# A two-layer hybrid decoder trunk on one core: first stage and layers in one block, modulation dealt to two engines

## The chip, the cores and the metric

The kernel runs on one core of a Trainium2 chip. A core has TensorE (PE) for matmuls, VectorE (DVE) and ScalarE (ACT) for elementwise work, GpSimd (POOL), and SyncE (SP), which issues most transfers; 16 DMA engines move the data. Each engine has its own queue of instructions, worked off in order, and waits on semaphores for the others. The metric is the device time of one execution in microseconds. The kernel before took 2327.58 us, the median of 3 runs (2323.72 to 2328.54).

## The reference

A trunk of two layers on x (1024 tokens, 1024 channels, float32). Before the layers, c gives six modulation vectors per layer; the first two (shift and scale of the first norm) are needed before anything else of a layer:

```python
ang = positions.astype(jnp.float32)[..., None] * inv_freq     # rotary angles
c_act = jax.nn.silu(c)
for l in range(DEPTH):                                        # 2 layers
    mod = c_act @ ada_w[l] + ada_b[l]                         # 1024 x 6144 weights
    sh1, sc1, g1, sh2, sc2, g2 = split(mod, 6)
    h = rmsnorm(x, norm1_g[l]) * (1.0 + sc1) + sh1
    proj = h @ w_in[l]
    y = concat(ssd_mixer, mla_mixer, swa_sink_mixer)(proj) @ w_out[l]
    x = x + g1 * y
    h = rmsnorm(x, norm2_g[l]) * (1.0 + sc2) + sh2
    u = causal_dwconv(h @ ffn_w_up[l])
    a, b = split(u, 2)
    x = x + g2 * ((silu(a) * b) @ ffn_w_down[l])
return rmsnorm(x, final_norm_g)
```

## The kernel before

Activations lie transposed on chip (channels on the 128 partitions, tokens along the row), as 8 tiles of 128 channels. A dense product of two float32 operands is made of three products of rounded parts: each operand is split into a high part (a copy by ACT) and a low part (a subtraction by POOL or DVE), and PE multiplies high by high, high by low and low by high. The weights of the input projection come in 20 packs of 128 columns, each loaded into one of two buffers (raw) and split. Everything is ordered by counted semaphores; the waits are written out by hand. In the layers a wait is given as `nth(name, v)`, v more than the count with which the layer began.

The program has three parts. The **first stage** is a block of its own. SP loads c, the rotary constants, the positions, the 8 tiles of x, tiles 0 to 7 of the modulation weights (`adaw`, 128 x 1024 each, 512 KB: tile i = 8 g + k holds rows 128 k to 128 k + 127 of vector g), then 16 narrow parameter loads (`load_params`, L394), tiles 8 to 15, and the first two packs of the input projection (`load_win`, L440); pack 0 consists of four narrow pieces. PE turns c, then the tiles of x one after another (L545), the copies out of its memory being made by ACT (L571); then it turns the parameters (L412 to L417), which waits for all 16 loads. ACT also squares x (L584), computes the sines (L586) and the roots of the norm (L588), and copies the parameters (L423). DVE computes the rotary angles (L606 to L617), then multiplies the modulation tiles by the silu of c and adds them up: tiles 1 to 7 into one sum, 9 to 15 into another (L625, L628). Tiles 0 and 8 are multiplied by PE itself, as products with one column (`part_sums`, L553), which also adds up the partitions of DVE's two sums in the same way. Between the two sums PE spreads the roots of the norm with 8 transposes (`spread_rms`, L453). DVE ends the stage with small additions (L638 to L641) and `first_modulation` (L431, L433). The two packs are split at the end (`split_ahead`, ACT L449, POOL L446).

The **second part** is a block in which the five engines clear the semaphores of the first. A block ends with all engines meeting. The **third** holds both layers (`trunk_layer`). Layer 0 starts with DVE's scaled norm (L2128), ACT's high part (L1743) and DVE's low part (L2136) of one channel tile after another, and PE's products of packs 0 and 1 with them (L1127), then packs 2 to 19 (L1067). SP's queue of layer 0 starts with eight further modulation tiles (L788), pack 2 and pack 3, and the store of x (L825).

Of the kernel before, what the change touches and what calls it, by code (L numbers as in the profile page):

```python
# [31 lines left out]
F32 = mybir.dt.float32  # L32
# [6 lines left out]
P = 128  # L39
T = 1024  # L40
# [89 lines left out]
ADA_GROUP = [0, 0, 1, 1, 2, 2, 3, 3, 4, 4, 4, 5, 5, 5, 6, 6]  # L130
# [47 lines left out]
def pv_end(u):  # L178
# [24 lines left out]
    "cum_stored": 16, "cum_loaded": 128, "ada_early_loaded2": 64, "sd_xe": 7, "sd_xe0": 1, "sd_t": 2, "sd_c": 4,  # L203
# [8 lines left out]


# [4 lines left out]
def build(nc, x, c, positions, ada_w, ada_b, norm1_g, norm2_g, w_in, ssd_conv_w, ssd_conv_b,  # L218
# [248 lines left out]
    adas = [place(f"adas{g}", [P, D], F32, E[(12, 13, 15)[g]]) for g in range(3)]  # L467
# [8 lines left out]
    with ExitStack() as st:  # L476
        s = sems(st, [f"x_loaded{t}" for t in range(NB // 2)] + [f"ada_loaded{i}" for i in range(7)] + ["small_loaded", "ident_ready", "pool_step", "x_transposed",
                      "x_copied_act", "x_copied_dve", "c_transposed", "c_act", "angle", "rope_sin",
                      "ada_done", "ada_sum", "dve_step", "params_loaded", "params_transposed", "params_copied", "mod_first",
                      "next_loaded0", "next_loaded1", "next_hi", "next_lo", "n1_sq", "n1_rstd", "n1_spread"])  # L480
        with nc.Block() as block:

            @block.sync
            def _(sp):
                sp.dma_start(crow[:], c.rearrange("b (k p) -> (b k) p", p=P)).then_inc(s["small_loaded"], 16)
                sp.dma_start(ropec[:], rope_consts).then_inc(s["small_loaded"], 16)
                sp.dma_start(posi[64:128, :], positions.to_broadcast([64, T])).then_inc(s["small_loaded"], 16)
                def load_adaw(i):
                    g, k = divmod(i, KT)
                    sp.dma_start(adaw[i][:], ada_w[0, k * P:(k + 1) * P, g * D:(g + 1) * D]).then_inc(s[f"ada_loaded{ADA_GROUP[i]}"], 16)  # L490

                for t in range(NB):
                    sp.dma_start(xin[t][:], x[0, t * P:(t + 1) * P, :]).then_inc(s[f"x_loaded{t // 2}"], 16)
# [11 lines left out]
            @block.gpsimd  # L505
            def _(pool):

                pool.memset(ident[:], 0.0).then_inc(s["pool_step"], 1)
                pool.memset(band[:], 0.0).then_inc(s["pool_step"], 1)
                pool.memset(caus01[:], 1.0).then_inc(s["pool_step"], 1)  # L510
                pool.memset(cs[0:64, :], 0.0).then_inc(s["pool_step"], 1)
                pool.memset(eps, EPS).then_inc(s["pool_step"], 1)
                pool.wait_ge(s["pool_step"], 5)
                pool.affine_select(out=ident[:], in_=ident[:], compare_op=ALU.not_equal, fill=1.0, base=0,
                                   pattern=[[-1, P]], channel_multiplier=1).then_inc(s["ident_ready"], 1)

                pool.affine_select(out=band[:, 0, :], in_=band[:, 0, :], compare_op=ALU.is_gt, fill=NEG, base=0,
                                   pattern=[[1, P]], channel_multiplier=-1).then_inc(s["ident_ready"], 1)

                pool.affine_select(out=band[:, 1, :], in_=band[:, 1, :], compare_op=ALU.is_ge, fill=NEG, base=0,  # L520
                                   pattern=[[-1, P]], channel_multiplier=1).then_inc(s["ident_ready"], 1)
                pool.affine_select(out=caus01[:], in_=caus01[:], compare_op=ALU.is_ge, fill=0.0, base=0,
                                   pattern=[[1, P]], channel_multiplier=-1).then_inc(s["ident_ready"], 1)
                for n in range(AHEAD):
                    split_ahead(pool, n)

            def x_copied(eng, t):

                if t < X_ACT:
                    eng.wait_ge(s["x_copied_act"], t + 1)  # L530
                else:
                    eng.wait_ge(s["x_copied_act"], X_ACT)
                    eng.wait_ge(s["x_copied_dve"], t + 1 - X_ACT)

            @block.tensor
            def _(pe):
                pe.wait_ge(s["ident_ready"], 4)
                pe.wait_ge(s["small_loaded"], 48)
                pe.transpose(bank[3][:, 0:8], crow[:], ident[0:8, 0:8]).then_inc(s["c_transposed"], 1)
                for t in range(NB):  # L540
                    pe.wait_ge(s[f"x_loaded{t // 2}"], 32)
                    if t >= 2:
                        x_copied(pe, t - 2)
                    for k in range(KT):
                        mm = pe.transpose(bank[t % 2][:, k * P:(k + 1) * P], xin[t][:, k * P:(k + 1) * P], ident[:])  # L545
                    mm.then_inc(s["x_transposed"], 1)
                x_copied(pe, NB - 1)
                transpose_params(pe, prow)

                def part_sums(a, column, weights):  # L550

                    for m in range(KT):
                        last = pe.matmul(bank[3][:, 16 + column + m:17 + column + m], a[:, m * P:(m + 1) * P], weights,  # L553
                                         start=True, stop=True)
                    last.then_inc(s["ada_sum"], 1)

                pe.wait_ge(s["c_act"], 1)
# [9 lines left out]
            def copy_x(eng, t, sem):  # L567
                eng.wait_ge(s["x_transposed"], t + 1)
                src = bank[t % 2][:].rearrange("p (k t) -> p k t", k=KT)
# [2177 lines left out]
```

## Time and profile before

| | before |
|---|---|
| median of 3 runs | 2327.58 us (2323.72 to 2328.54) |
| the profiled execution's own time | 2329.56 us |
| its span, first to last instruction | 2327.1 us |
| busy: PE, DVE, ACT, POOL | 2264.4, 1628.7, 1098.3, 1008.1 us |
| granted clock of PE, mean | 0.990 |
| first layer's first norm product | starts at 49.27 us |
| first dense product | starts at 51.61 us |

Times in the profile are microseconds from the start of the span unless they are marked as ns. L12 is line 12 of the kernel before. In a row of the timeline the start and the duration come first; `x16` means that 16 like instructions were merged, the duration then being from the start of the first to the end of the last; in square brackets stands how long the engine had been idle and what ended that. PEld is the loading of weights into PE. A granted clock of 1.00 is 2.4 GHz, 0.50 is 1.2 GHz.

### The profile page before, as it was taken

Reading aid. Unit: us, or ns where it says so; the run is one execution under the profiler, and the core shown is the slowest. Engines: PE = TensorE matmul, PEld = TensorE weight load, DVE = VectorE, ACT = ScalarE, POOL = GpSimd, SP = SyncE. Lnnn points to the kernel's source line nnn. Section 1 sums busy time; section 2 is a strip of 40 time slices with the busy share of each in tenths; the row PEclk is TensorE's granted clock in tenths of the full one; section 3 lists DMA queues with packets and bytes.
Section 4 is the critical chain, followed back from the end, with each engine's and each line's share of the span. In section 5 each row is a group of like instructions: output and inputs, shape, how many; then the busy total and the mean of one; then the engine's idle time right before and its main releaser. Section 6 shows DMA issues by size and latency. Waiting matters only on the chain.

```text
span 2327.1 us, 30806 instructions
## 1 busy us (share of the span) xinstructions
PE 2264.4 (97%) x11289; PEld 1833.2 (79%) x11289; DVE 1628.7 (70%) x2095; ACT 1098.3 (47%) x1808; POOL 1008.1 (43%) x641
## 2 busy tenths in 40 slices
PE   6999999999899999999999999999989999999998
PEld 5888866787788888888878787668878888888887
DVE  6885458449876666777888744672796767677886
ACT  4345546434444444444543464662444444444455
POOL 1222377444987777300012124043389777760000
PEclk7999999999999999999999999999999999999999
DMA  8742323342333333487557131004313333347763
GB/s 292 281 151 62 88 64 110 109 127 73 93 116 96 117 98 117 149 286 253 153 215 245 55 81 51 1 30 171 118 55 113 113 91 114 91 131 259 257 208 113
DMA packets 273012, 311.08 MB, mean 134 GB/s; under 512 B 37033, under 2 KB 191647, under 8 KB 271839
## 3 DMA queue, kind: packets, MB, share of 16 engines
q1 hardware_dynamic: 272174, 307.94, 40.7%
q8 instruction: 90, 1.47, 0.3%
q10 hardware_dynamic: 688, 1.18, 0.2%
q14 instruction: 60, 0.48, 0.1%
HBM read 246.53 MB, written 61.49 MB: 132 GB/s over the span
## 4 chain that ended last, share of the span: by engine, by line
PE 85%; DVE 7%; issue 2%; ACT 2%; POOL 1%; DMA 0%; DVEq 0%; SPq 0%; ACTq 0%; POOLq 0%
PE bank L1497 31%; PE bank L1067 18%; PE bank L1512 17%; PE bank L1127 6%; PE bank L1328 2%; PE bank L1360 1%; PE bank L1288 1%; DVE hLo L2150 1%; PE bank L1388 1%; DVE xT L2144 1%; PE bank L1217 1%; DVE xT L2472 1%; DVE tLo L2541 1%; ACT swaProb L1872 1%; PE bank L1195 1%
## 5 line engine op out<-in xcount | busy, mean ns | idle before, releaser
L987 POOL TENSOR_TENSOR wLo<-raw,wHi 128x1024 fp32r<-128x1024 f32 x66 | 161.5, 2448 | 411.4 <-ACT wHi L989 411.4
L1690 POOL TENSOR_TENSOR prodLo<-comb,prodHi 128x512 fp32r<-128x512 f32 x160 | 234.0, 1470 | 122.0 <-ACT prodHi L1029 122.0
L1497 PE MATMUL bank<-tHi,prodHi 128*128 128x512 f32 x640 | 249.9, 390 | 5.7 <-DVE tLo L2541 4.2
L1497 PE MATMUL bank<-tLo,prodHi 128*128 128x512 f32 x640 | 249.1, 389 | 0.0
L1497 PE MATMUL bank<-tHi,prodLo 128*128 128x512 f32 x640 | 249.1, 389 | 0.0
L1512 PE MATMUL bank<-gateHi,downHi 128*128 128x512 f32 x616 | 240.3, 390 | 0.0
L1512 PE MATMUL bank<-gateHi,downLo 128*128 128x512 f32 x616 | 239.7, 389 | 0.0
L1512 PE MATMUL bank<-gateLo,downHi 128*128 128x512 f32 x616 | 239.7, 389 | 0.0
L1029 ACT ACTIVATE prodHi<-comb 128x512 fp32r<-128x512 f32 x160 | 100.9, 634 | 249.0 <-PE bank L1497 228.7
L2486 DVE SCALAR_TENSOR_TENSOR ub<-bank,ffp,ub 128x1023 f32<-128x1023 f32 x88 | 112.8, 1282 | 141.9 <-ACT ub L1958 140.3
L1497 PE MATMUL bank<-hHi,prodHi 128*128 128x512 f32 x480 | 187.1, 390 | 7.1 <-POOL prodLo L1690 4.5
L1497 PE MATMUL bank<-hHi,prodLo 128*128 128x512 f32 x480 | 186.8, 389 | 0.0
L1497 PE MATMUL bank<-hLo,prodHi 128*128 128x512 f32 x480 | 186.7, 389 | 0.0
L1067 PE MATMUL bank<-hHi,wHi 128*128 128x512 f32 x576 | 184.8, 402 | 0.0
L1067 PE MATMUL bank<-hLo,wHi 128*128 128x512 f32 x576 | 178.2, 391 | 0.0
L1067 PE MATMUL bank<-hHi,wLo 128*128 128x512 f32 x576 | 177.5, 389 | 0.0
L989 ACT ACTIVATE wHi<-raw 128x1024 fp32r<-128x1024 f32 x66 | 69.7, 1059 | 219.1 <-PE bank L1067 144.5
L1690 POOL TENSOR_TENSOR prodLo<-raw,prodHi 128x512 fp32r<-128x512 f32 x120 | 165.0, 1405 | 0.0
L1497 PEld LDWEIGHTS bank<-tHi,prodHi 128*128 128x128 f32 x640 | 120.1, 188 | 33.1 <-DVE tLo L2541 5.0
L1497 PEld LDWEIGHTS bank<-tHi,prodLo 128*128 128x128 f32 x640 | 120.1, 188 | 25.2
L1497 PEld LDWEIGHTS bank<-tLo,prodHi 128*128 128x128 f32 x640 | 120.1, 188 | 24.8
L1512 PEld LDWEIGHTS bank<-gateHi,downHi 128*128 128x128 f32 x616 | 115.6, 188 | 24.4 <-issue 0.8
(393 smaller groups left out, 5346.4 us busy)
## 6 DMA issues: line engine op xcount, KB each, us to landing
raw<-in_ffn_w_up_dram SPq DMA_DIRECT2D x88, 512.0 KB, 4.8
gateRaw<-gateOut SPq DMA_DIRECT2D x154, 256.0 KB, 4.2
adaE<-in_ada_w_dram SPq DMA_DIRECT2D x64, 512.0 KB, 6.5
gateOut<-gateSums SPq DMA_DIRECT2D x22, 1024.0 KB, 5.5
raw<-in_w_in_dram SPq DMA_DIRECT2D x34, 512.0 KB, 4.1
downRaw<-in_ffn_w_down_dram SPq DMA_DIRECT2D x66, 256.0 KB, 3.8
raw<-in_w_out_dram SPq DMA_DIRECT2D x28, 512.0 KB, 3.8
downCols<-in_ffn_w_down_dram SPq DMA_DIRECT2D x24, 512.0 KB, 3.6
```

The source lines that it names most:

```text
L987: eng.tensor_tensor(lo[:], raw[slot][:], fview(hi[:]), ALU.subtract).then_inc(s["split_lo"], 1)
L989: eng.activation((early_hi if n in (N_OUT0, N_PRE + 2) else third_hi if n == 2 else wHi[slot])[:], raw[slot][:], ACT.Copy).then_inc(s["spl ...
L1029: act.activation(sHiW[idx][:], product_source(js, idx), ACT.Copy).then_inc(s["us_hi"], 1)
L1067: last = mm(half(pair, hf), w(k), r(k)[:, HALF * hf:HALF * (hf + 1)], start=first and q == 0, stop=last_k and q == 2)
L1127: last = mm(o, w[n % 2][:, k * P:(k + 1) * P], r(k)[:, cols], start=first and q == 0, stop=last_k and q == 2)
L1195: last = mm(half(3, 0)[:, g * 256:(g + 1) * 256], bt[:, g, :], xe[:, 4 * g:4 * g + 4, :], start=True, stop=True)
L1217: last = mm(o, xd[:, h, :], Mt[g][:, q, :], start=True, stop=True)
L1328: last = mm(bank[u % 2][:, q * HALF + a:q * HALF + b], qh[h][0:96, i * BLK:n], kh[h][0:96, a:b], start=True, stop=True)
L1497: last = mm(o, w[idx][:, c0], moving(idx, kp, hi), start=kp == 0 and q_ == 0, stop=kp == 3 and q_ == 2)
L1512: last = mm(down_bank(p, m), w[ring(n)][:, m * P:(m + 1) * P], g[ring(n)][:], start=i == 0 and q == 0, stop=i == NK - 1 and q == 2)
L1690: pool.tensor_tensor(sLoW[idx][:], product_source(js, idx), fview(sHiW[idx][:]), ALU.subtract).then_inc(s["us_lo"], 1)
L2486: dve.scalar_tensor_tensor(out=y[:, d:T], in0=bank[2 * q + b][:, 0:T - d], scalar=ffp[:, col:col + 1], in1=y[:, d:T], op0=ALU.mult, op1=AL ...
```

## The change

1. The first stage becomes a function, `first(block)`, that is called in the same block as the two layers; the block that cleared the semaphores is gone, and so are the ends of two blocks. The first stage uses semaphores of the layers under other names (`FIRST_ON`), and the layers count on from what it has left in them (`FIRST`, `passed`).
2. SP no longer issues the positions, the 16 parameter loads and pack 0; GpSimd's queue does, after its nine constants and before its splits. SP issues x, the 16 modulation tiles without a break, and pack 1.
3. Each modulation tile has its own semaphore. PE multiplies tiles 1, 3, 5, 7, 9, 11, 14 and 15; the eight transposes of `spread_rms` stand ahead of tile 9 in its queue. DVE multiplies and adds 0, 2, 4, 6 into one sum, 8, 10, 12, 13 into another, folds each by a 32 x 32 transpose and a reduction, and PE finishes the fold with four narrow products.
4. In layer 0 SP waits for the first modulation before the eight further modulation tiles. PE waits for the low part of pack 0 before its first product and of pack 1 before the second tile's, in both layers; SP's loads of packs 2 and 3 wait for the splits of packs 0 and 1 one by one. The early tiles' six semaphores become two.

```diff
-ADA_GROUP = [0, 0, 1, 1, 2, 2, 3, 3, 4, 4, 4, 5, 5, 5, 6, 6]
+ADA_BY_PE = (1, 3, 5, 7, 9, 11, 14, 15)
+ADA_BY_DVE = (0, 2, 4, 6, 8, 10, 12, 13)
...
 # SP, first stage
-                sp.dma_start(posi[64:128, :], positions.to_broadcast([64, T])).then_inc(s["small_loaded"], 16)
...
-                for i in range(8):
-                    load_adaw(i)
-                load_params(sp, lambda w: w[0:1], prow)
-                for i in range(8, 2 * KT):
-                    load_adaw(i)
-                for n in range(AHEAD):
-                    load_win(sp, w_in[0:1], n, n, s[f"next_loaded{n}"])
+            for i in range(2 * KT):
+                load_adaw(i)
+            load_win(sp, w_in[0:1], 1, 1, s["next_loaded1"])
...
 # GpSimd, after its constants
+            pool.dma_start(posi[64:128, :], positions.to_broadcast([64, T])).then_inc(s["pos_loaded"], 16)
+            load_params(pool, lambda w: w[0:1], prow)
+            load_win(pool, w_in[0:1], 0, 0, s["next_loaded0"])
...
 # PE, after the parameters' transposes
                 pe.wait_ge(s["c_act"], 1)
-                for g in range(2):
-                    pe.wait_ge(s[f"ada_loaded{ADA_GROUP[g * KT]}"], 16 * ADA_GROUP.count(ADA_GROUP[g * KT]))
-                    part_sums(adaw[g * KT], (2 + g) * KT, cact[:, 0:1])
-                pe.wait_ge(s["ada_done"], KT - 1)
-                part_sums(adas[0], 0, caus01[:, P - 1:P])
-                spread_rms(pe, "n1")
-                pe.wait_ge(s["ada_done"], 2 * KT - 2)
-                part_sums(adas[1], HALF, caus01[:, P - 1:P])
+            for n, i in enumerate(ADA_BY_PE):
+                if i == 9:
+                    spread_rms(pe, "n1")
+                pe.wait_ge(s[f"mod_loaded{i}"], 16)
+                part_sums(adaw[i], KT * n, cact[:, i % KT:i % KT + 1])
+            pe.wait_ge(s["ada_done"], len(ADA_BY_DVE) + 2)
+            for r in range(4):
+                last = pe.matmul(bank[0][32 * r:32 * r + 32, 0:2 * KT], quad[:], foldP[:].rearrange("p j c -> p (j c)")[:, r:2 * 32:4],
+                                 start=True, stop=True)
...
 # DVE
+            for n, i in enumerate(ADA_BY_DVE):
+                g, k = divmod(i, KT)
+                dve.wait_ge(s[f"mod_loaded{i}"], 16)
...
+                if n % 4 == 3:
+                    dve.wait_ge(s["ada_done"], n + 1 + g)
+                    link(dve.transpose(nt[2][:], adas[g][:]))
+                    dve.tensor_reduce(foldP[:, g, :], nt[2][:].rearrange("p (c i) -> p c i", i=32), AX.X, ALU.add).then_inc(s["ada_done"], 1)
...
+            dve.wait_ge(s["ada_sum"], len(ADA_BY_PE))
+            link(dve.tensor_reduce(mod[:, 0:2 * KT].rearrange("p (g m) -> p g m", g=2),
+                                   bank[3][:, 16:16 + KT * len(ADA_BY_PE)].rearrange("p (g n m) -> p g m n", g=2, m=KT), AX.X, ALU.add))
+            dve.wait_ge(s["params_copied"], 1)
+            link(dve.tensor_tensor(mod[:, 0:2 * KT], mod[:, 0:2 * KT], prm[:, R_ADAB:R_ADAB + 2 * KT], ALU.add))
+            dve.wait_ge(s["ada_sum"], len(ADA_BY_PE) + 1)
+            link(dve.tensor_tensor(mod[:, 0:2 * KT], mod[:, 0:2 * KT], bank[0][:, 0:2 * KT], ALU.add))
...
 # layers
-                if layer and n < AHEAD + 2:
-                    sp.wait_ge(s["next_hi"], nth("next_hi", 0))
-                    sp.wait_ge(s["next_lo"], nth("next_lo", 0))
+                if n < AHEAD + 2:
+                    sp.wait_ge(s["next_hi"], nth("next_hi", n - AHEAD - 1))
+                    sp.wait_ge(s["next_lo"], nth("next_lo", n - AHEAD - 1))
...
+                    else:
+                        sp.wait_ge(s["mod_first"], nth("mod_first", 0))
                     load_early(0, range(KT), 0)
...
-            if layer:
-                pe.wait_ge(s["next_lo"], nth("next_lo", 0))
...
+                if k == 0:
+                    pe.wait_ge(s["next_lo"], nth("next_lo", t - 1))
...
+    with nc.Block() as block:
+        first(block)
+        s.update(own)
+        passed.update(FIRST)
+        for layer in range(DEPTH):
+            trunk_layer(block, layer)
```

## Rows read from the trace of the kernel before

**Rows 1.** The page, part 4: the chain that ended last, by engine.

```profile
PE 85%; DVE 7%; issue 2%; ACT 2%; POOL 1%; DMA 0%; DVEq 0%; SPq 0%; ACTq 0%; POOLq 0%
```

**Rows 2.** The chain of waits from 0 to 130 us: start, duration, what.

```profile
51.61 24.81 PE bank L1127 x96
```

**Rows 3.** The timeline of DVE and POOL, end of the first stage.

```profile
42.91 4.66 POOL L446 TENSOR_TENSOR wLo<-raw,wHi 128x1024 fp32r<-128x1024 f32 x2 [39.31 <-ACT wHi L449]
...
46.59 0.16 DVE L641 TENSOR_TENSOR mod<-mod,bank 128x8 f32<-128x8 f32 x1 [3.45 <-PE bank L553]
46.79 0.81 DVE L431 TENSOR_TENSOR mod<-mod,prm 128x16 f32<-128x16 f32 x1
47.63 0.17 DVE L433 SCALAR_TENSOR_TENSOR scl<-mod,prm 128x8 f32<-128x8 f32 x1
49.27 1.40 DVE L2128 SCALAR_TENSOR_TENSOR nt<-xT,scl,bank 128x512 f32<-128x512 f32 x2 [1.48 <-PEq L645]
```

**Rows 4.** The timeline of SP and ACT, first 26 us.

```profile
1.68 0.57 SPq L487 DMA_DIRECT2D posi<-in_positions_dram  x1
...
23.82 1.05 ACT L571 ACTIVATE xT<-bank 128x1024 f32<-128x1024 f32 x1
...
25.93 1.05 ACT L586 ACTIVATE nt<-nt 64x1024 f32<-64x1024 f32 x1
```

**Rows 5.** The timeline of PE, 29 to 47 us.

```profile
29.22 0.44 PE L412 MATMUL bank<-ident,paramRows 121*128 121x121 f32 x1 [6.25 <-DMA paramRows<-in_ssd_a_log_dram]
...
30.83 6.99 PE L553 MATMUL bank<-cact,adaw 128*128 128x1 f32 x32
...
41.09 1.95 PE L453 MATMUL bank<-ident,rst 128*128 128x128 f32 x8
...
42.91 3.57 PE L553 MATMUL bank<-caus,adas 128*128 128x1 f32 x16
```

**Rows 6.** The timeline of DVE, 15 to 43 us.

```profile
15.30 0.69 DVE L617 TENSOR_SCALAR nt<-nt 64x1024 f32<-64x1024 f32 x1
...
20.95 8.23 DVE L628 SCALAR_TENSOR_TENSOR adas<-adaw,cact,adas 128x1024 f32<-128x1024 f32 x6 [1.73 <-DMA adaw<-in_ada_w_dram]
32.22 0.75 DVE L625 TENSOR_SCALAR adas<-adaw,cact 128x1024 f32<-128x1024 f32 x1 [3.03 <-DMA adaw<-in_ada_w_dram]
...
36.02 6.84 DVE L628 SCALAR_TENSOR_TENSOR adas<-adaw,cact,adas 128x1024 f32<-128x1024 f32 x5 [0.87 <-DMA adaw<-in_ada_w_dram]
```

**Rows 7.** Stretches: length; busy of PE, PEld, DVE, ACT, POOL; granted clock; DMA; GB/s.

```profile
408.50:411.90 3.40, 3.39 (x27) 2.68 (x27) 1.51 (x4) 1.62 (x5) 3.32 (x3) 0.99 0.00 0
411.90:415.10 3.20, 3.20 (x22) 2.42 (x24) 1.85 (x4) 1.50 (x2) 3.20 (x2) 0.50 0.00 0
...
19.30:22.70 3.40, 3.24 (x16) 2.83 (x15) 1.63 (x2) 3.40 (x6) 0.00 (x0) 0.50 1.03 410
22.70:26.40 3.70, 0.27 (x2) 0.00 (x0) 3.49 (x3) 3.68 (x7) 0.00 (x0) 0.96 1.04 354
...
30.80:46.50 15.70, 15.68 (x74) 15.31 (x74) 9.56 (x11) 2.73 (x6) 3.59 (x2) 0.50 0.74 225
```

**Rows 8.** The timeline of PE at 182 us and at 409 us.

```profile
182.72 0.30 PE L1144 MATMUL bank<-foldMod,quadSum 128*32 128x32 f32 x8
...
409.08 1.92 PE L1136 MATMUL bank<-caus,nt 128*128 128x1 f32 x16
410.86 0.96 PE L1360 MATMUL bank<-ident,prob 128*128 128x128 f32 x7
```

**Rows 9.** The timeline of DVE at 96 us: the transpose of one fold.

```profile
95.73 1.21 DVE L2197 STREAM_TRANSPOSE foldTurned<-nt 128x1024 f32<-128x1024 f32 x1
```

**Rows 10.** SP's parameter issues: timeline, then the line's groups (ns min/median/max).

```profile
20.44 0.59 SPq L394 DMA_DIRECT2D paramRows<-in_ssd_a_log_dram  x1
...
L394 SPq DMA_DIRECT2D paramRows<-in_norm_g_dram x2: 335/1034/1733, 11.6 to 12.0; - x2
...
L394 SPq DMA_DIRECT2D paramRows<-in_mla_q_norm_g_dram x1: 247/247/247, 15.3 to 15.3; - x1
```

More of the change, by code:

```diff
@@ L211 @@
     "dn_used": 69, "dn_full": 28, "dn_free": 16}
+FIRST_ON = {
+    "small_loaded": ("k_rope", 32), "ident_ready": ("up_base", 4), "pool_step": ("up_tap", 5),
+    "x_loaded0": ("gk_loaded0", 32), "x_loaded1": ("gk_loaded1", 32), "x_loaded2": ("gk_loaded2", 32), "x_loaded3": ("gk_loaded3", 32),
+    "x_transposed": ("up_silu", NB), "x_copied_act": ("up_mul", X_ACT), "x_copied_dve": ("g_sums", NB - X_ACT),
+    "c_transposed": ("dn_c", 1), "c_act": ("dn_copied", 1), "angle": ("dn_u", 1), "rope_sin": ("dn_pre", 1),
+    "ada_done": ("dn_used", 10), "ada_sum": ("us_c", 9)}
+FIRST_ON.update({f"mod_loaded{i}": (name, 16) for i, name in enumerate(
+    "dc_loaded0 dc_loaded1 dc_loaded2 g_stored0 g_stored1 g_stored2 x_back x_saved tail_loaded0 tail_loaded1 "
+    "sd_row_stored sd_spread uproj_loaded cum_stored dt_stored dt_loaded".split())})
+FIRST = {"dve_step": 16, "params_transposed": 1, "params_copied": 4, "mod_first": 1, "next_loaded1": 16, "next_hi": 2, "next_lo": 2,
+         "n1_sq": NB, "n1_rstd": 2, "n1_spread": 1}
+FIRST.update({name: count for name, count in FIRST_ON.values()})
 R_N1, R_N2, R_ADAB, R_CW, R_CB, R_SN, R_QN, R_KN, R_FN, R_DT, R_END = 0, 8, 16, 64, 96, 104, 108, 110, 111, 119, 121
@@ L466, in build @@
     adaw = [place(f"adaw{i}", [P, D], F32, at["h"] + 4 * K * i) for i in range(2 * KT)]
-    adas = [place(f"adas{g}", [P, D], F32, E[(12, 13, 15)[g]]) for g in range(3)]
+    adas = [place(f"adas{g}", [P, D], F32, E[12 + g]) for g in range(2)]
+    foldP = place("foldFirst", [P, 2, 32], F32, E[15])
     two_pi = 6.283185307179586
@@ L684, in build @@
         up_base up_tap up_silu up_mul g_stored0 g_stored1 g_stored2 g_sums gk_loaded0 gk_loaded1 gk_loaded2 gk_loaded3 dc_loaded0 dc_loaded1 dc_loaded2 dn_c dn_copied dn_u dn_pre g_hi g_lo dn_used dn_full dn_free""".split()
+    names += "turned x_gained made_act made_dve out_written".split()
+    held = ExitStack()
+    s = sems(held, names + ["first_pos", "first_params", "first_win0"])
+    own = {n: s[n] for n in s}
+    s.update({signal: own[name] for signal, (name, count) in FIRST_ON.items()})
@@ L1234, in scan_after @@
                         6: [(scan_back, ch)] + ([(scan_turn, ch + 1)] if ch + 1 < NB else [])}
[L1236 to L1237 removed]
             for t, k in [(t, k) for t in range(2) for k in range(4)] + [(t, k) for k in range(4, KT) for t in range(2)]:
[L1239 to L1240 removed]
+                if k == 0:
+                    pe.wait_ge(s["next_lo"], nth("next_lo", t - 1))
+                    if layer:
+                        pe.wait_ge(s["dn_free"], nth("dn_free", -1 if t else -3))
                 pe.wait_ge(s["n1_lo"], nth("n1_lo", n1_done(0, k)))
@@ L2238, in key_rope @@
                     rope(dve.tensor_tensor(misc[a, :], misc[a, :], misc[b, :], ALU.add), 3)
-            early_products(0, range(KT), 0, KT)
+            early_products(0, range(KT), 0)
             step_sum()
@@ L2243, in _ @@
             mod_fold(0)
-            early_products(1, range(KT), 1, KT)
+            early_products(1, range(KT), 1)
             mod_fold(1)
@@ L2268, in _ @@
                 if j == 0:
-                    early_products(2, range(4), 2, 4)
+                    early_products(2, range(4), 2)
                 if j == 1:
@@ L2700, in _ @@
                 made_by_dve(6)
-    names += "turned x_gained made_act made_dve out_written".split()
-    with ExitStack() as st:
-        s = sems(st, names)
-        with nc.Block() as block:
-            for layer in range(DEPTH):
-                trunk_layer(block, layer)
-                for name, count in PER_LAYER.items():
-                    passed[name] = (layer + 1) * count
+    with nc.Block() as block:
[4 more added lines that the diff above has]
+            trunk_layer(block, layer)
+            for name, count in PER_LAYER.items():
+                passed[name] = FIRST.get(name, 0) + (layer + 1) * count
 _INS = ["x", "c", "positions", "ada_w", "ada_b", "norm1_g", "norm2_g", "w_in", "ssd_conv_w", "ssd_conv_b",
```

294 lines of the change are left out of this document (132 added, 162 removed), and 3 rows, old and new, of the table PER_LAYER.

## The prediction

> **What bounds the kernel now.** I read the page first, then the chain of waits from the start, then the first 60 us of the timeline engine by engine, and last the granted clock in stretches of that time. The page's chain lies on TensorE (PE) for 85% of the span [rows 1]. The chain from the start shows where PE takes over: at 51.61 us the first dense products begin and PE goes on without a gap for 24.81 us, and then with the next packs [rows 2]. So whatever the first stage takes is added to the span whole: no engine has slack behind 51.61 us that could swallow it. The change is almost all in front of that point, and I measure it by one moment, the start of VectorE's (DVE's) first norm product (L2128), at 49.27 us before [rows 3]. From there to the first dense product is 2.34 us of DVE, ScalarE, DVE, which the diff leaves alone.
>
> What comes before 49.27: DVE sums 14 of the 16 tiles of the modulation weights (tiles 9 to 15 wait for their transfers, 3.03 us and 0.87 us, the last five go through by 42.86) [rows 6]; PE turns the second sum in 16 one-column passes, 42.91 to 46.48 [rows 5]; DVE closes with three small operations; then 1.48 us of nothing until L2128, which is the end of the block, the clearing of the semaphores and the second end [rows 3]. Two of the terms are known at sight: the barriers, 1.48 us, and 0.64 us of L431, which took 0.81 us for 16 columns and ended at 47.60, when GpSimd's split (42.91 + 4.66 = 47.57) let go [rows 3].
>
> **The change part by part.**
>
> *Barriers.* Gone: -1.48 us. Counted offsets cost nothing: the same waits with other constants. L2128 waits for mod_first and n1_spread, both signalled just before.
>
> *Modulation on PE.* This is the large term. PE had 2 of the 16 tiles and two turned sums; it now has 8 tiles. One tile is 8 products, and each is two passes of a weight load and a one-column matmul: 32 passes for two tiles took 6.99 us, so 3.5 us a tile; the two sums of 16 passes took 3.57 us the second time, the same [rows 5]. DVE pays 1.37 us for such a tile (6 in 8.23 us) [rows 6]. Eight tiles on PE are 28.0 us in one queue, in order. PE cannot start them before it has transposed x and the parameters. The last copy of x that it waits for ends at 23.82 + 1.05 = 24.87 us; without the positions' issue in front of x (0.57 us on SP's queue) it is 24.3 [rows 4]. Then:
>
> - parameters ready: 25.2, see below
> - their transposes: 29.19 to 30.83 before, 1.64 us [rows 5]: 26.8
> - tiles 1, 3, 5, 7: 14.0: 40.8. All landed (DVE ran through 0 to 7 by 29.2 [rows 6])
> - the eight turns of the norm's roots now stand in the middle of PE's queue, 1.9 us [rows 5]: 42.7. Their input, the reciprocal behind tile 8, is there by 33
> - tiles 9, 11, 14, 15: 14.0: 56.7. Tiles 11 to 13 had landed at 36.02, and DVE went on through 14 and 15 without a wait [rows 6], so no transfer ends last here
> - the fold of DVE's half, eight narrow passes: 0.30 us at 2.4 GHz for the like of it [rows 8], doubled for 1.2 GHz: 57.3
> - DVE's add and scale: 0.11 to start, 0.16, 0.04, 0.17 [rows 3], and L2128 follows: 57.8. The reduction of PE's 64 columns and the bias run beside the fold.
>
> 57.8 against 49.27: +8.5 us. The barriers and L431's stall are already in that difference.
>
> *The clock.* All of that stands on the 3.5 us of a tile, which is the price at a granted clock of 0.50 (1.2 GHz). At full clock 16 one-column passes took 1.78 us (409.08 to 410.86) [rows 8]. What would raise it? In 30.80:46.50 PE was busy 15.68 of 15.70 us, nearly all with such passes, and had 0.50 throughout. In 19.30:22.70 it was at 0.50 too, with full transposes, and had 0.96 behind that, in 22.70:26.40. In 408.50:411.90 PE was busy 3.39 of 3.40 us at 0.99, with 16 one-column passes in it, and had 0.50 in the 3.2 us behind [rows 7]. So one-column passes neither raised the clock nor held it. I take 0.50 from 26.4 us on, as before. A start of the parameters' transposes at full clock would give back up to 0.8 us.
>
> The Trainium skill, "TensorE: Matmul & The Clock Gate", Part 1, has the clock follow how busy the engine has been, and full rate come with sustained matmul activity. By that rule 28 us of matmuls without a gap would run at full rate and the change would win, as in the first rival below; this trace disagrees, with 15.68 us busy at 0.50.
>
> *DVE's half.* Eight tiles (2 x 0.75 + 6 x 1.37), two 32x32 transposes (1.21 us each [rows 9]) and two reductions of as many columns (taken the same), the scaled sines and the reciprocal: about 15.6 us. It starts behind DVE's chain for the sines, which ended at 15.30 + 0.69 = 16.0 [rows 6] and ends some 2 us later with later positions. Tile 13 is there at 36.0, then 1.3 + 2.4: finished at 40 to 43. PE needs it at 56.7, so it costs nothing; if PE were at full clock it would be late together with PE's own last tile.
>
> *Narrow transfers on GpSimd's queue.* Positions, 16 parameter loads and the four loads of weight pack 0 leave SP. Before, PE waited 6.25 us for the last parameter row, issued from 20.44 to 21.03 and landed by 29.2 [rows 5, 10]; that wait goes, which is in the sum. No row shows a DMA issued by GpSimd. Lower bound: SP's issues, 0.25 us the shortest; 17 of these from 3.6 us on land long before 24.3, and nothing is exposed. Upper bound: 1.73 us, the longest [rows 10], 17 times from 3.6, and 8.2 us to land: 41 us, 16 us late. I take the parameters at 25.2, nearest to SP's case (all 16 issued in the 9.4 us from 11.6 to 21.0 [rows 10]), with 0.9 us of exposure for a slower queue. Page price: the Trainium skill, "DMA: Bandwidth & Descriptors", gives about 1 us to the first byte on this path; by it 17 issues are out at 21 us and the sum is the one above. The positions only have to be in by 14 us, since ScalarE gets to the sines at 25.93 [rows 4] and DVE's chain in front of them is 10.7 us. Pack 0's slivers used to be in by 42, since GpSimd's share of the two splits ran from 42.91 for 4.66 us [rows 3]; the first product now starts at 60: over 12 us of cover. If they share the transfer engines with tiles 14 and 15, these may land at 42 to 44; PE reaches tile 14 at 49.7.
>
> *SP's queue in layer 0.* The wait for mod_first puts the eight early loads at the moment where the block used to put them, beside L2128; pack 2 and the store of x are queued behind them as before. No change relative to L2128. In layer 1 the looser waits on the split packs (one of two) release nothing that the chain waits for there. Shared semaphores for the early tiles: same order, same data.
>
> **Sum.** Profiled execution 2329.56 us, span 2327.1: +8.5 gives 2338 and 2335.6. The median of the three runs is 2327.58, 2.0 under the profiled one; to it the sum is 2336.1.
>
> **Rivals.**
> *1. PE's passes run at full clock (faster).* Start 25.2, transposes 0.9, four tiles 7.1, roots 1.0: 34.2; tiles 9 and 11: 37.8; 14 and 15: 41.4, or 43.4 if tile 15 lands at 41.6, when DVE read it; fold and close 0.8: 42.2 to 44.2, 5 to 7 us ahead of 49.27. 2321.5. For it: the queue has no gap, and the clock was high in 22.70:26.40. Against it: the two stretches with one-column passes [rows 7]. It decides as soon as the clock is high for more than about 60% of the 28 us; the break-even is 8.5 us saved of the 13.8 that full clock would save.
> *2. GpSimd's queue issues the 17 transfers late (slower still).* Over 1.2 us each, PE starts later than 25.2 one for one; at 1.73 us, 41 us, it is +24: 2352; at 1.4 us with 5 us to land, 32 us, +15.5: 2343. For it: 17 issues in a row on an engine whose price no row shows. Against it: SP's average of 0.59 us.
> The skill's "SBUF — State Buffer" (the trap of DVE blocking a GpSimd DMA) says that such a DMA stands still while DVE is in its two-port mode. No row here shows it; by it the issues beside DVE's fast operations from 6 to 18 us would be among the late ones.
> *3. No change.* PE gets a part of the time at full clock, some 40 to 60% of it, and the gain meets the loss: 2325 to 2331.
>
> **How the numbers follow.** Forecast 0.80, with its own range 2333.5 to 2341 (0.8 us of clock at the start, parameters from hidden to 5 us late). Rival 1: 0.09. Rival 2: 0.06. Rival 3: 0.05. About 0.2%, 4.7 us, is what a measurement can tell from no change here. The range leaves out rivals 1 and 3 and the far end of 2: 2332 to 2343. Faster 0.09, same 0.05, slower 0.86.
>
> **What would show it.** Right: PE busy without a gap from 25 to 57 us at a granted clock of 0.50, 16 passes in 3.5 us; L2128 at about 58 us; DVE's last fold at 40 to 43; no idle DVE between L433's like and L2128; the chain behind the first dense product shifted by a constant. Wrong: a clock of 1.00 in 27:57, a PE that waits for parameters beyond 27 us, or a first dense product that waits for pack 0.

## The result, and the profile after

The changed kernel takes 2331.91 us (median of 20 runs, 2328.77 to 2336.78), the kernel before 2325.62 on the same chip (20 runs, 2322.66 to 2331.80). The ratio is 1.0023, 95% interval 1.0016 to 1.0031: slower by 5.3 us, or by 6.3 us if the medians are subtracted. The prediction said slower, 2336.1 us in 2332.0 to 2343.0; the time lies 0.09 us below the range. The profiled execution of the changed kernel took 2330.20 us, with a span of 2328.2.

The moment by which the prediction measured, the first norm product (L2128), moved from 49.27 us [rows 3] to 55.53, by 6.26 us, where 8.5 was forecast. First the timeline of PE in the changed kernel, 21 to 56 us (start, duration, line, operation, output and inputs; in brackets the idle time before it and what ended it), which answers to [rows 5]:

```profile
23.80 0.32 PE L425 MATMUL bank<-ident,paramRows 121*128 121x121 f32 x1 [2.75 <-ACT xT L600]
...
25.27 13.82 PE L580 MATMUL bank<-cact,adaw 128*128 128x1 f32 x64
38.94 1.95 PE L466 MATMUL bank<-ident,rst 128*128 128x128 f32 x8
40.68 13.65 PE L580 MATMUL bank<-cact,adaw 128*128 128x1 f32 x64
54.26 0.30 PE L592 MATMUL bank<-foldFirst,quadSum 128*32 128x16 f32 x8
```

This is the queue that the prediction wrote down, without a gap from 23.80 to 54.5 us: parameters, four tiles, the eight turns, four tiles, the fold. Their order and kind are right, and each is a little shorter than forecast. The first row shows that the transposes of the parameters wait for ScalarE's copy of x, and no longer for a parameter row (before, 6.25 us for the transfer [rows 5]).

The stretches (length; busy time of PE, PEld, DVE, ACT, POOL; granted clock; DMA share; GB/s), answering to [rows 7]:

```profile
19.30:22.70 3.40, 1.06 (x8) 0.85 (x8) 3.30 (x4) 3.40 (x6) 0.00 (x0) 1.00 1.02 255
22.70:26.40 3.70, 2.60 (x25) 2.40 (x25) 2.35 (x3) 3.66 (x7) 0.00 (x0) 0.68 1.02 409
25.30:54.30 29.00, 29.00 (x142) 28.98 (x142) 14.00 (x13) 4.63 (x9) 4.70 (x2) 0.50 0.61 231
```

PE is busy 29.00 of 29.00 us and is granted 0.50 (1.2 GHz) all the while. Just before, in 19.30:22.70, it was at 1.00 with PE busy 1.06 of 3.40 us. The first rival needed full clock here and is out.

VectorE (DVE), its folds and its close, answering to [rows 3, 6]:

```profile
41.08 1.25 DVE L663 STREAM_TRANSPOSE nt<-adas 128x1024 f32<-128x1024 f32 x1
42.36 1.22 DVE L664 TENSOR_REDUCE foldFirst<-nt 128x32 f32<-128x1024 f32 x1
54.37 0.22 DVE L672 TENSOR_REDUCE mod<-bank 128x16 f32<-128x64 f32 x1 [10.79 <-PE bank L580]
54.63 0.17 DVE L675 TENSOR_TENSOR mod<-mod,prm 128x16 f32<-128x16 f32 x1
54.84 0.17 DVE L677 TENSOR_TENSOR mod<-mod,bank 128x16 f32<-128x16 f32 x1
55.04 0.17 DVE L678 SCALAR_TENSOR_TENSOR scl<-mod,prm 128x8 f32<-128x8 f32 x1
55.53 1.41 DVE L2128 SCALAR_TENSOR_TENSOR nt<-xT,scl,bank 128x512 f32<-128x512 f32 x2 [0.32 <-DVE scl L678]
```

DVE has finished its half at 43.58 and stands still for 10.79 us until PE has its last tile. That is the change in one number: half of the tiles went to the engine that needs 3.4 us for one, and the engine that needs 1.3 waits. The 1.48 us in front of L2128 [rows 3] are 0.32 now, and L431's 0.81 is 0.17.

GpSimd's queue, answering to [rows 10]; of the 16 parameter issues the first group and the last:

```profile
3.55 0.72 POOL L548 DMA_DIRECT2D posi<-in_positions_dram  x1
4.26 1.05 POOL L407 DMA_DIRECT2D paramRows<-in_norm_g_dram  x2
...
11.97 0.89 POOL L407 DMA_DIRECT2D paramRows<-in_ssd_a_log_dram  x1
12.85 4.10 POOL L453 DMA_DIRECT2D raw<-in_w_in_dram  x4
```

All 17 are out at 12.86 us, 0.55 us each, and the last parameter row lands 5.5 us after its issue, so the parameters are in long before PE asks for them.

**Only the first stage differs.** Before, the first dense product stood at 51.61 us [rows 2]; it is at 57.96 now. From there to the up-projection of the queries in layer 0 it is 258.27 us before and 258.19 after. Later in this pair of profiles the offset shrinks, to 5.0 us at the norm of layer 1 and to 1.1 us at the end of the span, while the medians of 20 runs each differ by 6.3: behind the first 310 us single executions part from each other by some us (from the up-projection to the end of the span the profiles of this document have 2011.6 to 2017.7 us), and a difference of 1.1 in two spans would have misled. So the experiments are compared by two things, their place at 310 us and their ratio over many runs.

### The profile page after: what moved, and what is told of

It is laid out like the page before. It is cut to its first block, busy times and chain, and to the rows that moved or that the text cites. A ratio compares the mean times of both kernels' runs of the same rounds, so it can differ in the third digit from the quotient of the medians.

```text
span 2328.2 us, 30890 instructions
## 1 busy us (share of the span) xinstructions
PE 2273.1 (98%) x11361; PEld 1843.8 (79%) x11361; DVE 1621.0 (70%) x2092; ACT 1096.3 (47%) x1808; POOL 1021.6 (44%) x662
## 4 chain that ended last, share of the span: by engine, by line
PE 87%; DVE 7%; ACT 2%; issue 2%; POOL 1%; DMA 1%; SPq 0%; DVEq 0%; ACTq 0%; POOLq 0%
PE bank L1497 31%; PE bank L1067 18%; PE bank L1512 18%; PE bank L1127 6%; PE bank L1328 2%; PE bank L1360 1%; PE bank L1288 1%; PE bank L580 1%; DVE hLo L2150 1%; PE bank L1388 1%; DVE xT L2144 1%; PE bank L1217 1%; DVE xT L2472 1%; DVE tLo L2541 1%; ACT swaProb L1872 1%
## 5 line engine op out<-in xcount | busy, mean ns | idle before, releaser
L1497 PEld LDWEIGHTS bank<-tHi,prodLo 128*128 128x128 f32 x640 | 120.4, 188 | 25.2
```

The source lines that it names most:

```text
L1497: last = mm(o, w[idx][:, c0], moving(idx, kp, hi), start=kp == 0 and q_ == 0, stop=kp == 3 and q_ == 2)
```

## The experiments

The times of each in one table. "Norm" is the start of the first norm product, "dense" that of the first dense product, "up" that of the up-projection of the queries in layer 0, all from one profile, in us.

| kernel | norm | dense | up | ratio to before, interval |
|---|---|---|---|---|
| before | 49.27 | 51.61 | 309.88 | 1 |
| changed | 55.53 | 57.96 | 316.15 | 1.0023 [1.0016, 1.0031] |
| e_blocks | 47.96 | 50.40 | 308.58 | 0.9992 [0.9983, 1.0002] |
| e_queue | 48.89 | 51.33 | 309.48 | 1.0002 [0.9993, 1.0011] |
| e_mod | 60.58 | 63.02 | 321.18 | 1.0041 [1.0027, 1.0054] |
| e_deal4 | 48.09 | 50.52 | 309.06 | 1.0006 [0.9997, 1.0014] |
| e_dense | 69.87 | 72.30 | 330.47 | 1.0078 [1.0059, 1.0097] |
| e_dense4 | 73.37 | 75.81 | 334.30 | one run, 2354.0 us |
| e_front4 | 46.44 | 49.10 | 307.39 | 0.9997 [0.9986, 1.0008] |
| e_front4p | 49.47 | 51.90 | 310.20 | 1.0004 [0.9992, 1.0015] |
| e_front4x | 47.41 | 49.85 | 308.24 | 0.9997 [0.9987, 1.0008] |
| e_port | 43.85 | 48.12 | 306.28 | 0.9989 [0.9978, 1.0000] |
| e_defer | 43.66 | 46.09 | 306.12 | 0.9994 [0.9985, 1.0003] |

"Up" minus "dense" is 258.15 to 258.54 in all but e_defer (260.03), so up to that point a shift of the first stage is carried on one for one. The shifts of "up" lie within the intervals of the ratios for all but two kernels: e_deal4 (-0.8 us, interval -0.7 to +3.3) and e_defer (-3.8, interval -3.5 to +0.7) are just outside. On the whole the times moved by somewhat less than the shifts. Why, stays open.

### The parts one by one: e_blocks, e_queue, e_mod

e_blocks keeps the joined block and puts the rest back: narrow transfers on SP, the old deal.

```
+            sp.dma_start(posi[64:128, :], ...)         # first on SP, as before
+            load_params(sp, ...)                       # behind tile 7, as before
-            for n, i in enumerate(ADA_BY_PE): ...
+            (two tiles and two turned sums on PE, 14 tiles on DVE, as before)
```

> The changed kernel with the narrow transfers back on SP's queue and the modulation dealt as before, so that only the joined block is left. Measure: start of the layers' first norm product on DVE (L2128 of before), 49.27 us before, 55.53 changed. Theory A (the 28 us of one-column passes in PE's queue at 1.2 GHz are the whole loss; joining the blocks gains the barriers): 47.8 us, time 1.5 us below before, ratio 0.9994. Rival B (GpSimd's queue is the loss): also 47.8, B is tested by the next run. Rival C (counting on shared semaphores in one block costs what the barriers did): 49.3 or more.

> The joined block and GpSimd's queue, modulation dealt as before (14 tiles on DVE, 2 on PE). A: parameters turned by 25.3 us, but DVE's sines now end at 23.0 instead of 16.0, so its 14 tiles run without waiting from 23.0 to about 43; first norm product at 47.5 (47 to 49), ratio 0.9993. B (the narrow packets slow the wide transfers, and DVE starts too late): 52 us or later, above before.

e_queue has the joined block and GpSimd's queue, with the old deal.

> The joined block and the new deal of the modulation, narrow transfers back on SP's queue. A: the parameters land at 29.2 us as before, and PE's queue starts from there: 29.2 + 1.6 + 14.0 + 1.9 + 13.8 + 1.2 = 61.7 us for the first norm product, ratio 1.0053; so the queue alone gained 6 us of what the deal lost. B: 55.5 us or less, since the slow queue is gone.

e_mod has the joined block and the new deal, with the narrow transfers on SP.

What was measured, by the start of the first norm product:

- the joined block alone: -1.31 us, as expected (47.96 for 47.8)
- GpSimd's queue on top of it: +0.93 with the old deal. A gain was expected (47.5, measured 48.89), since PE no longer waits for the parameters. That wait is gone, but the tiles land later, and DVE, which waits for them, now ends last (rows below). DVE also starts late: positions issued at 3.55 us beside the loads of x are waited for until 10.85, where SP's were there at 5.24. That is not what ends last, though, since DVE waits for transfers again behind its sines
- GpSimd's queue with the new deal: 60.58 to 55.53, -5.05, because PE is last in both and starts its tiles at 25.27 in place of 30.32
- the new deal: +12.62 without the queue, +6.64 with it

The wait for tile 10 and the tiles behind it, in e_blocks, then in e_queue:

```profile
32.49 1.28 DVE L658 SCALAR_TENSOR_TENSOR adas<-adaw,cact,adas 128x1024 f32<-128x1024 f32 x1 [0.42 <-DMA adaw<-in_ada_w_dram]
34.58 6.84 DVE L658 SCALAR_TENSOR_TENSOR adas<-adaw,cact,adas 128x1024 f32<-128x1024 f32 x5
...
35.33 1.28 DVE L656 SCALAR_TENSOR_TENSOR adas<-adaw,cact,adas 128x1024 f32<-128x1024 f32 x1 [0.40 <-DMA adaw<-in_ada_w_dram]
37.42 6.84 DVE L656 SCALAR_TENSOR_TENSOR adas<-adaw,cact,adas 128x1024 f32<-128x1024 f32 x5
```

Tile 10 comes 2.84 us later. Pack 0, 0.5 MB, now goes ahead of it, 1.3 us at the 410 GB/s that the loads reach. And while GpSimd's transfers run, the engines are as busy but move less: 322 GB/s in 8:12 us and 262 in 18:22, against 412 and 410 in e_blocks. How the 2.84 us divide between the two was not tested.

So the two edits can't be priced one at a time: the queue costs 0.9 or gives 5.1, by whether DVE's tiles or PE's end the stage. The new deal is the loss, in both settings.

### Fewer tiles on PE: e_deal4

```
-ADA_BY_PE = (1, 3, 5, 7, 9, 11, 14, 15)
+ADA_BY_PE = (1, 5, 11, 15)
+ADA_BY_DVE = (0, 2, 3, 4, 6, 7, 8, 9, 10, 12, 13, 14)
```

> The changed kernel with 4 tiles on PE (1, 5, 11, 15, the norm's spread ahead of 11) and 12 on DVE, six in each sum. A: PE has 7.0 us of passes less before the spread and again 7.0 behind it; tile 11 to 41.1, tile 15 to 44.6, DVE's second fold by 44.5; first norm product at 45.8 us (45 to 47.5), ratio 0.9985 to before. B: no better than 53 us, because the parameters and positions come as late as in the changed kernel.

The first norm product comes 7.4 us earlier than in the changed kernel, at 48.09. PE is done with its tiles at 45.63 in place of 54.33, although it now waits 4.22 us for DVE's reciprocal in front of the turns. So the price of a tile on PE is shown: four tiles less are 13.6 us less of passes. It is 2.3 us later than expected (and outside the 45 to 47.5), since DVE is now last. Rows of PE, then of DVE:

```profile
36.89 1.97 PE L466 MATMUL bank<-ident,rst 128*128 128x128 f32 x8 [4.22 <-DVE rst L670]
38.66 6.97 PE L580 MATMUL bank<-cact,adaw 128*128 128x1 f32 x32
46.95 0.31 PE L592 MATMUL bank<-foldFirst,quadSum 128*32 128x16 f32 x8 [1.32 <-DVE foldFirst L664]
...
31.75 1.78 DVE L658 SCALAR_TENSOR_TENSOR adas<-adaw,cact,adas 128x1024 f32<-128x1024 f32 x1 [1.51 <-DMA adaw<-in_ada_w_dram]
45.68 1.22 DVE L664 TENSOR_REDUCE foldFirst<-nt 128x32 f32<-128x1024 f32 x1
```

DVE's sines end at 22.22, but what holds it is again a transfer: the tile at the end of its first sum is there only at 31.75, takes 1.78 us in place of 1.28 beside GpSimd's split of pack 0 (29.24 to 32.45), and from there DVE works without a pause until its second fold ends at 46.90.

### What the clock does: e_dense and e_dense4

After each of PE's eight tiles one product, or four, that nothing reads:

```
                 part_sums(adaw[i], KT * n, cact[:, i % KT:i % KT + 1])
+                for _ in range(1):          # 4 in e_dense4
+                    pe.matmul(half(3, 1)[:, 0:512], ident[:], xin[0][:, 0:512], start=True, stop=True)
```

> The changed kernel with one matmul more after each of PE's eight modulation tiles: 128x512 fp32, a product that nothing reads, into a corner of bank 3. It asks whether columns that stream lift the granted clock that stands at 0.50 while PE is busy with one-column passes. If they do, the 16 passes (two tiles' worth of 64) cost 0.11 us a matmul and less from there on, tiles of 1.8 us with dense matmuls of about 0.9: PE's tiles end near 48 and the first norm product starts near 50. Rival: the clock stays at 0.50, each dense matmul adds 1.7 us at that clock, and the first norm product starts near 69, some 13 us after that of the changed kernel (55.5).

> The changed kernel with four matmuls of 128x512 after each of PE's eight tiles in place of one (nothing reads them): 7.3 us of streaming for each 3.4 us of one-column passes at half clock. If the share of streaming is what lifts the granted clock, it goes to 1.00 within the first tiles and the stage is shorter than at half clock: dense products of 0.9, passes of 1.8, first norm product between 70 and 95. Rival: it stays at 0.50 and the eight tiles take 8 x 10.8 = 86 us: first norm product near 114, some 58 us after that of the changed kernel.

One product for each tile (e_dense) changed nothing in the clock. Here are two tiles of its timeline and the stretch around them (a product shows as x2, since each is done in two passes):

```profile
53.23 3.41 PE L580 MATMUL bank<-cact,adaw 128*128 128x1 f32 x16
56.51 2.05 PE L591 MATMUL bank<-xin,ident 128*128 128x512 f32 x2
58.35 3.41 PE L580 MATMUL bank<-cact,adaw 128*128 128x1 f32 x16
...
48.00:60.00 12.00, 12.00 (x47) 9.93 (x45) 0.00 (x0) 0.00 (x0) 0.00 (x0) 0.50 0.00 1
```

The rival held: 69.87 against its 69. With four (e_dense4) the clock was at 0.50 from 25 to 33.7 us, at 0.93 in 33.70:35.00, with PE in the last of the first four products, and at 1.00 from there on:

```profile
25.24 3.58 PE L580 MATMUL bank<-cact,adaw 128*128 128x1 f32 x16
28.68 6.27 PE L591 MATMUL bank<-xin,ident 128*128 128x512 f32 x8
34.78 1.84 PE L580 MATMUL bank<-cact,adaw 128*128 128x1 f32 x16
36.48 3.68 PE L591 MATMUL bank<-xin,ident 128*128 128x512 f32 x8
...
40.00:50.00 10.00, 10.00 (x48) 6.42 (x47) 2.87 (x3) 1.06 (x1) 2.34 (x1) 1.00 0.14 38
```

The same 16 passes stand there at two prices, 3.58 and 1.84 us, and PE is busy without a gap in both. Seven of its eight tiles ran at full clock, so the first rival's arithmetic was sound; what it lacked was a reason for the clock to rise. As a remedy it is none: the four products cost more (3.5 us a tile at full clock) than the passes save (1.7): the stage is 17.8 us longer than in the changed kernel.

The Trainium skill, "TensorE: Matmul & The Clock Gate", Part 1, has the clock follow how busy the engine is. The runs do not bear that out as it stands: 29.00 of 29.00 us busy at 0.50 in the changed kernel, 12.00 of 12.00 at 0.50 in e_dense, 10.00 of 10.00 at 1.00 in e_dense4.

### The stage rearranged: e_front4, e_front4p, e_front4x

From e_deal4: positions first on SP, and both packs behind the last tile on SP.

```
+            sp.dma_start(posi[64:128, :], positions.to_broadcast([64, T]))...   # SP, ahead of x
-            pool.dma_start(posi[64:128, :], ...)
-            load_win(pool, w_in[0:1], 0, 0, s["next_loaded0"])                  # stays in e_front4p
+            for n in range(AHEAD):
+                load_win(sp, w_in[0:1], n, n, s[f"next_loaded{n}"])             # e_front4, e_front4x
-X_ACT = 8
+X_ACT = 6                                                                       # e_front4x only
```

> The joined block with four tiles on PE (1, 5, 11, 15) and twelve on VectorE, as the run of before this one, but positions issued first on SP, both packs by SP after the last tile, and GpSimd's queue with the parameters alone. VectorE's sines should end near 16 and not 23, its tiles then wait for the transfers and not for VectorE, the last of them lands near 38 and the fold ends near 42; PE's four tiles and spread end near 42 too. First norm product at 43.5 (42.5 to 45.5), against 49.3 of before: ratio 0.9975, about 2320.5. Rival: what the first norm product gains is not kept, because the packs (which now land last, near 41) and their splits are late for the first projection, or a later stage waits for its own transfers: first norm product near 43.5 and a ratio of 0.999 or more.

> As e_front4, but pack 0 stays on GpSimd's queue, in the midst of the tiles. It takes 0.5 MB of bandwidth ahead of the last tiles, so they land 1.3 us later and the first norm product starts near 44.8; if that product is what counts, the ratio is 0.9980. If the packs decide, this one is the better of the two.

> As e_front4, with the last two x copies on VectorE. ScalarE's copies and squares end PE's transposes at 23.8; with two copies less (0.92 each) PE starts its tiles about 2 us earlier, at 23.4, while VectorE, which waits for transfers, takes the copies in its idle time. If the last tile's landing decides, the first norm product stays near 43.5 and the ratio is that of e_front4; if PE was last, it comes to 42.

Positions by SP land at 5.22 us, DVE's sines end at 15.9, and the stage then goes by the transfers: PE's last tile waits for its landing at 39.6. e_front4p, with 0.5 MB more in front of the tiles, is 3.0 us later than e_front4 (1.3 was expected). DVE's second fold ends 5.4 us later there: the wait for tile 6 ends at 31.15 in place of 26.84, and GpSimd's split of pack 0, at 30.08, holds DVE up for another 1.1 us; in return the stall shown below is missing. e_front4x gains nothing: PE starts its tiles 2.9 us earlier, at 24.13, but the two copies take DVE's time, and its second fold ends at 44.21 in place of 42.87. The ratio of e_front4 is 0.9997 where 0.9975 was expected; part of that is that it came at 46.44 and not at 43.5. Its timeline of DVE and GpSimd at the end of the stage shows where 2 of these 2.9 us are:

```profile
43.47 0.18 DVE L675 TENSOR_TENSOR mod<-mod,prm 128x16 f32<-128x16 f32 x1
43.69 0.17 DVE L677 TENSOR_TENSOR mod<-mod,bank 128x16 f32<-128x16 f32 x1
43.89 2.23 DVE L678 SCALAR_TENSOR_TENSOR scl<-mod,prm 128x8 f32<-128x8 f32 x1
46.44 1.41 DVE L2128 SCALAR_TENSOR_TENSOR nt<-xT,scl,bank 128x512 f32<-128x512 f32 x2 [0.32 <-DVE scl L678]
...
43.75 4.66 POOL L459 TENSOR_TENSOR wLo<-raw,wHi 128x1024 fp32r<-128x1024 f32 x2 [30.66 <-ACT wHi L462]
```

An operation of eight columns takes 2.23 us, and ends where the first of GpSimd's two splits does (43.75 + 2.33 = 46.08). It is the stall that L431 had before, 0.81 us [rows 3], grown, since the stage now ends earlier and the splits don't.

### The stall: e_port and e_defer

e_port gives the last operations one input from PSUM each:

```
-            link(dve.tensor_reduce(mod[:, 0:2 * KT]..., bank[3]...))
+            link(dve.tensor_reduce(bank[1][:, 0:2 * KT]..., bank[3]...))
-            link(dve.tensor_tensor(mod, mod, prm[...], ALU.add))
+            link(dve.tensor_tensor(mod, bank[1][:, 0:2 * KT], prm[...], ALU.add))
+            link(dve.tensor_tensor(bank[1][:, 64:64 + KT], bank[0][:, KT:2 * KT], mod[:, KT:2 * KT], ALU.add))
...
-            dve.scalar_tensor_tensor(out=scl, in0=mod[:, KT:2 * KT], ...
+            dve.scalar_tensor_tensor(out=scl, in0=bank[1][:, 64:64 + KT], ...
```

> As e_front4, where the last operation of the modulation (scale from mod and the parameters, 128x8, both in SBUF) took 2.23 us and ended with GpSimd's first split, against 0.17 elsewhere. Theory: VectorE's operations with two SBUF inputs wait until GpSimd's split, which also reads SBUF, has ended. So here the last operations each read one input from PSUM, with one operation more. The scale operation then takes 0.2 and starts at 44.1; the first norm product (one PSUM input) starts at 44.6 in place of 46.4; but the first hLo (two SBUF inputs) waits until the split ends near 46.1, or the second near 48.5, so PE's first product starts at 47 at best, against 49.1: ratio 0.9985 to 0.9995. Rival: the 2.23 us is the issue of the operation and not the operands; it stays 2 us, and so does the first norm product at 46.4.

```profile
43.37 0.17 DVE L680 SCALAR_TENSOR_TENSOR scl<-bank,prm 128x8 f32<-128x8 f32 x1
43.85 1.41 DVE L2130 SCALAR_TENSOR_TENSOR nt<-xT,scl,bank 128x512 f32<-128x512 f32 x2 [0.32 <-DVE scl L680]
45.65 2.32 DVE L2138 SCALAR_TENSOR_TENSOR hLo<-nt,mod,hHi 128x512 fp32r<-128x512 f32 x1 [0.39 <-ACT hHi L1745]
...
42.63 4.80 POOL L459 TENSOR_TENSOR wLo<-raw,wHi 128x1024 fp32r<-128x1024 f32 x2 [29.28 <-ACT wHi L462]
```

The same operation, with one input from PSUM, takes 0.17 us in the midst of a split (42.63 to 47.43). The next one with two inputs in SBUF, hLo, takes 2.32 in place of 0.75 and ends 0.5 us behind the split. So it is the second SBUF input that waits for GpSimd. The Trainium skill, "SBUF — State Buffer", in "Who interferes with whom", states this rule: a DVE instruction with two SBUF inputs contends with a GpSimd instruction that reads SBUF, and one with a single SBUF input, outside the two-port modes, doesn't; these rows agree. The rival, that the operation's issue takes the 2 us, is out. Of the 2.6 us that the first norm product gains over e_front4 only 1.0 reaches the dense product, at 48.12 (49.10 there), because hLo now waits; the ratio is 0.9989.

e_defer keeps the second split back until four hLo are made, and lets PE take five k of pack 0 first:

```
-            for n in range(AHEAD):
-                split_ahead(pool, n)
+            split_ahead(pool, 0)
+            pool.wait_ge(s["n1_lo"], 4)
+            split_ahead(pool, 1)
...
 # PE, layers: in layer 0 five k of pack 0 come first, in place of four
+            early = 4 if layer else 5
```

> As e_port, and GpSimd's second split (pack 1) starts only when VectorE has made four hLo; PE takes the first five k of pack 0 before it needs pack 1 (four before). In e_port the first hLo (two SBUF inputs) took 2.32 us and ended 0.5 us after the second split. Theory of the two inputs: here the first split ends near 45, the first hLo takes 0.75 and PE's first product starts at 46.2 (48.1 in e_port, 51.6 before); the fifth hLo waits 2 us instead, while PE has earlier work. From PE's first product to the first product of the up-projection of the queries is 258.2 us in nearly every run, so that one starts near 304.4, 5.5 us before that of the kernel before; ratio 0.9978, 2321. Rival: the wait moves to the fifth hLo and PE stands still for it, so that up-projection starts near 306, as in e_port, and the ratio stays near 0.9989.

The first dense product does come at 46.09, and the stall does move to the fifth hLo (50.98, 2.29 us). The rival held: PE's fifth k of pack 0 needs just that hLo.

```profile
51.36 0.63 PE L1130 MATMUL bank<-hHi,wLo 128*128 128x512 f32 x1
53.33 0.50 PE L1130 MATMUL bank<-hHi,wHi 128*128 128x512 f32 x1 [1.34 <-DVE hLo L2140]
```

The up-projection starts at 306.12, 0.16 us ahead of e_port. e_port has the lowest ratio found: clearly faster than the changed kernel, and 2.6 us (0 to 5.1) faster than the one before. The intervals of e_front4 and e_defer overlap with its own, so the times don't tell these versions apart.

## Why the prediction was right in direction and 4.2 us too high

The mechanism held, and the time came out below the range because terms of the sum were too large: the start of PE's tiles, the price of a tile, and the median from which the sum began. Measured against the prediction's own steps:

| step | predicted | measured |
|---|---|---|
| PE free for the parameters | 25.2 | 23.80 |
| their transposes | 1.64 | 1.47 |
| first four tiles | 14.0 | 13.67 (25.27 to 38.94) |
| turns of the roots | 1.9 | 1.74 |
| last four tiles | 14.0 | 13.58 (40.68 to 54.26) |
| fold | 0.6 | 0.30 |
| close, to L2128 | 0.5 | 0.97 |
| L2128 | 57.8 | 55.53 |

- **The mechanism** held in every step: eight tiles of one-column passes in PE's queue at half clock, without a gap, with DVE done at 43.6 ("40 to 43") and waiting for PE, the barriers' 1.48 and L431's stall gone, and everything from the dense product to 310 us moved by a constant. e_mod against e_blocks and the changed kernel against e_queue show that the deal alone makes the loss.
- **The step that was mis-sized most is PE's start**, 25.2 us for a measured 23.80. The 0.9 us of exposure for a slower GpSimd queue was not there: 17 issues of 0.55 us were out at 12.86 us, and the transposes waited for ScalarE's copy. That copy ended at 23.74 and not at 24.3. The sum had taken off only the 0.57 us in which SP issues the positions, and not their transfer: with these 256 KB no longer ahead of x, ScalarE's first copy of x starts at 8.89 us, before at 10.19. It starts at 8.62 to 8.89 in the five profiles with the positions on GpSimd and at 9.85 to 10.65 in the eight with them ahead of x. Together 1.4 us. The transposes themselves ran partly at full clock (0.17 less).
- **A tile** was taken at 3.5 us, by dividing rows that overlap; start to start it is 3.41. Eight of them: 0.75 us.
- **The close** was under-priced by 0.47. For 0.32 of it L2128 did not follow L678 at once, a gap that the sum put at nothing; for the rest the reduction of PE's columns and the bias ran on for 0.24 us behind the fold, since both wait for PE's last tile. The fold's 0.30 less makes up for most of it. Start, transposes, tiles, turns, fold and close together are 2.27 us of the 4.2.
- **The baseline** is the rest, 2.0 us: the three runs shown had a median of 2327.58 (the prediction's base), the 20 beside the changed kernel 2325.62. 2325.6 + 6.3 is the measured time.
- **The first rival** fell by the clock, 0.50 for 29 us. e_dense shows that busy time does not lift it, e_dense4 that it would have halved the tiles. The second fell by the issues of 0.55 us. The prediction's page price took a time to the first byte for the time of an issue, and came to 21 us for a measured 12.86. The sentence beside that rival, on issues that stand still beside DVE's fast operations, hardly came into play here, since DVE ran nothing before 11.66 us; only the last issue, at 11.97, met DVE's work and took 0.89 us. e_front4 shows the size: with DVE's TENSOR_SCALAR operations beside them, 6.4 to 9.4 us, four of the issues took 0.73 to 0.80 us, which took 0.50 to 0.51 in the changed kernel. What was late on GpSimd's queue was the landing of the positions (11.66 us). They were in time for ScalarE ("in by 14 us"), but DVE's sines ended 7.0 us later than before, at 23.01, and not 2. PE ended last, so it cost nothing.
- **The range** was too narrow on the low side. Below the 2336.1 stood only the 0.8 us for the clock at the start and the 0.9 us of exposure (2334.4, written as 2333.5), and then 2332 to leave "no change" out. An earlier x, a cheaper tile, and the 2 us of uncertainty of a median over three runs were not in it. That the direction came out right is no luck; that the time missed the range by 0.09 us and not by more is.

What stays open: by their ratios the times follow the shifts at 310 us by a little less than one for one (5.3 of 6.3 us in the changed kernel, 18.1 of 20.6 in e_dense), and the profiles don't tell where it is given back, since single executions differ behind 310 us by as much.

## What to carry to other kernels

Price a matrix-vector product on PE by its passes, at the clock that the trace shows for such passes, and give PE only as many of them as end together with the other engine: here, at 3.4 us for a tile against 1.3 on DVE, four of sixteen tiles on PE ended 1.3 us before DVE's fold, and eight 10.8 us behind it. Numbers between were not tried. An edit that frees a wait is worth its time only on the engine that ends the stage, so two edits that change who is last have to be priced together. When a stage gets shorter, look for what doesn't move with it: GpSimd's splits, harmless before but for 0.6 us, took 2 us from the shorter versions.

## What the runs showed of the hardware

- One-column fp32 passes kept the granted clock at 0.50 for 29 us of unbroken work; four 128x512 products for each 16 passes brought it to 1.00 and the passes from 3.4 to 1.7 us start to start.
- GpSimd issued 17 transfers in 9.3 us, 0.55 us each. A 256 KB transfer of positions that it issued at 3.55 us, beside SP's loads of x, was waited for until 11.66; issued by SP at 1.69, ahead of x, it was there at 5.22 (e_front4).
- Beside GpSimd's transfers the DMA engines were as busy (1.02 to 1.07) and moved less: 322 and 262 GB/s in e_queue against 412 and 410 in e_blocks, in 8:12 and 18:22 us.
- DVE operations with two SBUF inputs stood still during GpSimd's subtraction of two SBUF tiles, for up to 2.1 us in an operation that takes 0.17; one with a PSUM input went through at once. Where DVE's operation had started first the split was the longer one: 3.21 us in e_deal4 for the 2.35 of the changed kernel.
